# Hybrid decoder block on eight cores: own tokens' copy later, new unit orders, eight banks for the down projections

## Chip, cores and metric

One Trainium2 chip, all 8 cores, one launch. Each core computes 1024 of the 8192 token rows; nothing is exchanged between cores. The metric is the device time of the slowest core in microseconds. The engines are TensorE (PE), VectorE (DVE), ScalarE (ACT), GpSimd (POOL) and SyncE (SP); POOL and SP issue the DMAs.

## The reference

Two sequences of 4096 tokens, width 2048, one layer (cut; the causal convolutions `causal_dwconv3` have three taps):

```python
u = rmsnorm(h, ln1_g)
z = u @ w_in           # zb | zc | zv | q_lat 768 | kv_lat 512 | k_rope 64 | gates
y_conv = (zb * causal_dwconv3(zc * zv, conv_w)) @ w_conv_out
q = (rmsnorm(q_lat, q_a_g) @ w_q_b).reshape(b, s, 16, 192)
kv = (rmsnorm(kv_lat, kv_a_g) @ w_kv_b).reshape(b, s, 16, 256)   # k_nope 128 | v 128
k = concat([k_nope, broadcast(k_rope)])
q = apply_rope_tail(rmsnorm(q, q_norm_g), cos, sin)
k = apply_rope_tail(rmsnorm(k, k_norm_g), cos, sin)
y_mla = causal_attention(q, k, v) @ w_mla_out
h = h + (sigmoid(gate_a) * y_conv + sigmoid(gate_b) * y_mla) @ w_o
u = rmsnorm(h, ln2_g)
a_gate, a_up = split(causal_dwconv3(u @ w_ffn_up, ffn_conv_w) + ffn_conv_b)
h = h + (silu(a_gate) * a_up) @ w_ffn_down
```

## The kernel before

A small scheduler (`Sched`) takes operations in program order, one list per engine, and derives every semaphore wait from the buffers that an operation reads and writes. Each engine runs its list in order. That holds for the DMA issues of SP and POOL too: an issue that waits holds up what stands behind it in the list.

**Chunk stage (lines 476 to 666).** All 4096 keys of the core's sequence go through in eight groups `g` of 512. `load_x(g)` (POOL, four quarters, three buffers) brings the transposed tokens as bf16. TensorE multiplies them with the key/value input weights `wkv_sb` (loaded as f32 by four SP DMAs `wq_ops`, scaled on VectorE) into five PSUM banks `z[0]` to `z[4]`; `ssq` sums squares into `pss`, and `p2` holds the sums of the latent. The eight banks rotate, seven a group, so the next group's second bank is this group's `z[0]`. VectorE then evicts: `ea`, `fkv`, four latents `cT` (line 642), the rotary key, and the own tokens. `krss_mm(g)` (line 577), put off into the next group by `pend`, sums the rotary key's squares into the bank `p2` and copies them out on VectorE.

The own tokens of group `g` (128 of the 512) are also loaded in f32: `load_own(g)` on SP into the single buffer `xown` (`Txo`), `own_gain` multiplies by the gain in place (line 566), and line 651 writes their normalized bf16 copy into slot `7 - g` of `u_own`. `load_pos(g)` on SP fills the single buffer `posi`; `rope_tables` (line 508) reads it in its first instruction, a cast, and builds the angles for the next group in ten VectorE instructions. In group `g` SP's order before is `load_pos(g+1)`, `load_own(g+1)`; the first is free to go as soon as the cast for group `g` has read `posi`.

**Query latents (lines 673 to 709).** Three query tiles `t` = 2, 1, 0 of 260, 390 and 390 columns (two slots, three, three: tile 2 reads slots 7 and 6, tile 1 slots 5 to 3, tile 0 slots 2 to 0), six latent chunks `i` of 16 matmuls each. The sums of tile `t+1` (`qstats`) come after the first chunk of the next tile. The weight ring (`wpump`, four slots, POOL) is filled ahead of this.

**First head (lines 1051 to 1056).** `prologue_units(0)`: `KU` (512 keys: matmuls, VectorE copy, ScalarE square), `KF` (sums of squares of 2048 keys, after which the second one gives the key scale), `VU` (512 values, VectorE copy), `QA`, `QB`, `QC`, `QD` (a query tile: projections, sums, normalization). `qstats(0)` stands behind the second unit.

**Attention (lines 1061 to 1114).** 16 heads of 32 key steps, each with the score matmuls, an exponential on ScalarE, masks on POOL and the value matmuls. The 27 projection units of head h+1 are spread one a step over head h, in one PSUM bank to step 13, two from 14, three from 26; steps 2, 14 and 26 hold transposes instead. At the end of the units `u_end` releases the head's two weight blocks, and `wpump` puts the loads of two later ones on POOL.

**Convolution mixer, gates, output projection, FFN.** In the FFN `ups(g)` and `downs(g)` alternate (`FFN_ORDER`: up 0, up 1, down 0, up 2, down 1, up 3, down 2, down 3). An up pass has six projections in banks 0 to 5, then the three-tap convolution on VectorE. A down pass has 16 chunks of two halves, 11 matmuls each, in the banks `p = 6 + half`, and each half is added into `hres` by VectorE (line 1286).

Of the kernel before, what the change touches and what calls it, by code (L numbers as in the profile page):

```python
# [6 lines left out]
F32 = mybir.dt.float32  # L7
# [3 lines left out]
AF = mybir.ActivationFunctionType  # L11
# [175 lines left out]
BH = 132  # L187
# [80 lines left out]
def build_program():  # L268
# [216 lines left out]
    def load_x(g, deps=()):  # L485
        b = g % 3
        for q in range(4):
            src = xk[g * 128:(g + 1) * 128, q * 4 * NT:(q + 1) * 4 * NT].rearrange("p (k n) -> p k n", n=NT)
            S.add(POOL, lambda e, src=src, dst=xb[b][:, 4 * q:4 * q + 4, :]: e.dma_start(out=dst, in_=src),  # L489
                  writes=[Txb[b][q]], chan="x%d%d" % (b, q), extra_deps=deps)  # L490
# [9 lines left out]
    load_x(0)  # L500
# [28 lines left out]
    load_own(0)  # L529
# [35 lines left out]
    def own_gain():  # L565
        tt(xown, xown, C("g1", 0, 16).unsqueeze(2).broadcast_to([128, 16, 128]), ALU.mult, [Txo, Tcst], [Txo])

# [18 lines left out]
    own_gain()  # L586
    sqx(0, 0)
    sqx(0, 1)
    for g in range(NG):
# [51 lines left out]
        for m in range(4):  # L641
# [9 lines left out]
        tt(u_own[:, :, s * BH + 4:s * BH + BH], xown, r_[:, 0:128].unsqueeze(1).broadcast_to([128, 16, 128]),  # L651
           ALU.mult, [Txo, Tr_], [Tu[s]])
        if g + 1 < NG:
            load_pos(g + 1)
            load_own(g + 1)
            if g == 0:
                halo()
            rope_tables(posi, Tposi, NT)
            own_gain()
# [5 lines left out]
        if g == 2:  # L665
            S.add(POOL, lambda e: e.dma_start(out=msk, in_=mskd), writes=[Tmsk], chan="msk")
    load_wql(4, Twk)
    load_wql(5, Twk)
    wstate["cap"] = NSLOT
    wstate["deps"] = [S.last[DVE], S.last[ACT], S.last[PE]]  # L670
    wpump()
# [25 lines left out]
    for t in (2, 1, 0):  # L697
        b = t % 2
        off, n = QT[t]
        for i in range(6):  # L700
# [3 lines left out]
            if t == 2 and i == 0:  # L704
                pend.pop(0)()
            if i == 0 and t < 2:
                qstats(t + 1)
            act(qlatf[b][:, i, 0:n], PS[p][:, 0:n], AF.Copy, [TP[p]], [Tqlf[b][i]])
# [53 lines left out]
    for i_ in range(NPT):  # L762
        S.add(DVE, lambda e, i_=i_: e.memset(PH[i_], 1.0), writes=[TPc[i_]])
        S.add(DVE, lambda e, i_=i_: e.memset(PT[i_], 0.0), writes=[TPa[i_], TPb[i_]])  # L764
# [5 lines left out]
    later = []  # L770

# [8 lines left out]
    def prologue_units(h):  # L780
# [29 lines left out]
        def VU(g):  # L810
# [7 lines left out]
            cp(Vh[hb][:, 4 * g:4 * g + 4, 0:128], slots(PS[p], 128), [TP[p]], [TVh[hb][g]])  # L818
# [37 lines left out]
        if h == 0:  # L856
            units = [lambda: (u_start(), KU(0)), lambda: KU(1), lambda: KU(2), lambda: KU(3), lambda: VU(0),
                     lambda: KF(0), lambda: KU(4), lambda: KU(5), lambda: KU(6), lambda: KU(7), lambda: VU(1),
                     lambda: KF(1)]
            units += [lambda g=g: VU(g) for g in range(2, 8)]  # L860
            for t in (2, 1, 0):
                units += [lambda t=t: QA(t), lambda t=t: QB(t), lambda t=t: QC(t)]
            return units + [u_end]
        units.append(lambda: (u_start(), KU(0)))
        for ct in range(1, 4):
            units.append(lambda ct=ct: KU(ct))
        units.append(lambda: VU(0))
        units.append(lambda: KF(0))
        for ct in range(4, 8):
            units.append(lambda ct=ct: KU(ct))  # L870
        units.append(lambda: VU(1))
        units.append(lambda: KF(1))
        for t in range(3):
            units.append(lambda t=t: QA(t))
            units.append(lambda t=t: QB(t))
            units.append(lambda t=t: VU(2 + t))
            units.append(lambda t=t: QC(t))
        for g in range(5, 7):
            units.append(lambda g=g: VU(g))
        units.append(lambda: (VU(7), u_end()))  # L880
# [170 lines left out]
    for i_, u in enumerate(prologue_units(0)):  # L1051
        u()
        run_later()
        if i_ == 1:
# [6 lines left out]
    for si, (h, kb) in enumerate(steps):  # L1061
# [12 lines left out]
        while nq < len(steps) and nq <= si + 3:  # L1074
# [13 lines left out]
            nq += 1  # L1088
        if later:
# [183 lines left out]
    def downs(g):  # L1273
        gb = g % 2
        for c in range(16):
            wd, Twd = wget(("fd", g, c))
            h3 = slots(hres[:, c, :], BQ)
            for half in range(2):
                p = 6 + half
# [135 lines left out]
```

How the kernel before makes its waits and increments, by code:

```python
        def replay(e, eng):  # L149
            sem_e = sched.eng_sem[e]
            for o in sched.ops[e]:
                for (sem, v) in o.waits:
                    eng.wait_ge(sem, v)
                ins = o.fn(eng)
                if o.is_dma:
                    ins.then_inc(sched.chan_sem[o.chan], 16)
                elif o.needs_inc:
                    ins.then_inc(sem_e, 1)
# [18 lines left out]
            @block.sync  # L177
            def _(eng):
                replay(SP, eng)
                for ch in final_waits:
                    eng.wait_ge(sched.chan_sem[ch], 16 * sched.chan_cnt[ch])
```

## Time and profile before

| | us |
|---|---|
| median of 3 runs | 2735.43 (2735.18 to 2775.98) |
| profiled execution | 2735.31 |
| its span, slowest core (core 0) | 2733.8 |
| spans of the eight cores | 2729.8 to 2733.8 |

The span runs from the first to the last instruction. A line of the timeline has the start, the busy time and the instruction, with the count behind an x; the bracket at its end is the idle time of the engine before it and what ended it. A list of waits has the waiting engine and what it waited for, the total, the count and the longest. In a table of stretches each engine has its busy microseconds and its instructions in brackets, then the granted TensorE clock (1.00 is 2.4 GHz), the DMA engines' share and GB/s.

### The profile page before, as it was taken

Reading aid. Unit: us, or ns where it says so; the run is one execution under the profiler, and the core shown is the slowest. Engines: PE = TensorE matmul, PEld = TensorE weight load, DVE = VectorE, ACT = ScalarE, POOL = GpSimd, SP = SyncE. Lnnn points to the kernel's source line nnn. Section 1 sums busy time; section 2 is a strip of 40 time slices with the busy share of each in tenths; the row PEclk is TensorE's granted clock in tenths of the full one; section 3 lists DMA queues with packets and bytes.
Section 4 is the critical chain, followed back from the end, with each engine's and each line's share of the span. In section 5 each row is a group of like instructions: output and inputs, shape, how many; then the busy total and the mean of one; then the engine's idle time right before and its main releaser. Section 6 shows DMA issues by size and latency. Waiting matters only on the chain.

```text
span 2733.8 us, 54684 instructions; the slowest of 8 cores (2729.8 to 2733.8 us)
## 1 busy us (share of the span) xinstructions
PE 2630.4 (96%) x19779; PEld 1670.5 (61%) x19938; DVE 1241.0 (45%) x1966; ACT 844.3 (31%) x1349; POOL 505.8 (19%) x1355
## 2 busy tenths in 40 slices
PE   6998899999999999999999999999999999999999
PEld 2445566666666766666666666666665466456544
DVE  5784443443443442322211223367776277457622
ACT  3663566666666665211111111110000000000000
POOL 1100143443443433300000000000000100100010
PEclk9999999999999999999999999999999999999999
DMA  9962010010010011345444545544444444444457
GB/s 212 167 127 49 11 21 12 12 21 12 12 21 12 12 27 25 55 77 117 70 80 68 82 74 117 111 75 71 73 75 68 79 78 73 64 81 71 67 82 174
DMA packets 55268, 186.92 MB, mean 68 GB/s; under 512 B 6240, under 2 KB 6368, under 8 KB 53472
## 3 DMA queue, kind: packets, MB, share of 16 engines
q0 software_dynamic: 47088, 150.26, 34.1%
q1 hardware_dynamic: 7920, 33.15, 3.6%
q8 instruction: 168, 2.75, 0.4%
q14 instruction: 92, 0.75, 0.1%
HBM read 325.24 MB, written 8.39 MB: 122 GB/s over the span
## 4 chain that ended last, share of the span: by engine, by line
PE 91%; DVE 3%; DMA 3%; issue 2%; ACT 1%; POOL 0%; SPq 0%; DVEq 0%; ACTq 0%; POOLq 0%
PE ps L326 49%; PE pw L326 43%; DMA arena<-wkvin 1%; DVE arena L333 1%; DVE arena L350 1%; ACT arena L330 1%; DVE arena L337 1%; DMA arena<-xk 1%; DMA arena<-xo 0%; DMA outT<-arena 0%; POOL arena L347 0%; DVE arena L343 0%; DVE arena L764 0%; DVEq L153 0%; POOL arena L489 0%
## 5 line engine op out<-in xcount | busy, mean ns | idle before, releaser
L326 PE MATMUL ps<-arena 128*128 128x129 bf16 (+8 forms) x12121 | 1480.6, 275 | 64.0 <-DVE arena L350 22.4
L326 PE MATMUL pw<-arena 128*128 128x390 bf16 (+5 forms) x7658 | 1313.1, 321 | 35.3 <-DVE arena L341 21.4
L326 PEld LDWEIGHTS ps<-arena 128*128 128x128 bf16 x12202 | 967.5, 98 | 565.3 <-issue 99.8
L326 PEld LDWEIGHTS pw<-arena 128*128 128x128 bf16 x7736 | 730.7, 98 | 493.4 <-issue 41.5
L337 DVE TENSOR_TENSOR arena<-ps,arena 128x512 f32<-128x512 f32 (+6 forms) x475 | 252.7, 535 | 792.3 <-PE ps L326 714.0
L330 ACT ACTIVATE arena<-pw,arena 128x1024 bf16<-128x1024 f32 (+9 forms) x608 | 428.3, 712 | 484.5 <-PE pw L326 444.5
L330 ACT ACTIVATE arena<-arena 128x512 bf16<-128x512 bf16 (+8 forms) x381 | 269.8, 715 | 947.0 <-DVE arena L333 726.4
L397 POOL DMA_DIRECT2D arena<-wall x288 | 167.8, 583 | 1551.6 <-PE ps L326 1162.9
L347 POOL TENSOR_TENSOR arena<-arena 128x128 bf16<-128x128 bf16 (+1 forms) x1024 | 317.7, 334 | 461.6 <-ACT arena L330 459.3
L333 DVE SCALAR_TENSOR_TENSOR arena<-arena 128x1024 f32<-128x1024 f32 (+6 forms) x309 | 311.8, 1013 | 121.0 <-ACT arena L330 94.4
L350 DVE CAST arena<-ps 128x512 bf16<-128x512 f32 (+2 forms) x311 | 193.9, 634 | 260.6 <-PE ps L326 260.0
L337 DVE TENSOR_TENSOR arena<-pw,arena 128x390 f32<-128x390 f32 (+5 forms) x245 | 129.0, 555 | 140.3 <-PE pw L326 130.4
L337 DVE TENSOR_TENSOR arena<-arena 128x390 bf16<-128x390 f32 (+5 forms) x173 | 162.2, 937 | 54.1 <-ACT arena L330 32.1
L330 ACT ACTIVATE arena<-ps 128x390 bf16<-128x390 f32 (+8 forms) x215 | 99.7, 467 | 119.4 <-PE ps L326 116.1
L343 DVE TENSOR_SCALAR arena<-arena 128x1024 f32<-128x1024 f32 (+2 forms) x106 | 79.3, 748 | 1.9
L330 ACT ACTIVATE arena<-pw 128x512 bf16<-128x512 f32 (+7 forms) x60 | 29.1, 506 | 101.6 <-PE pw L326 97.8
L341 DVE TENSOR_SCALAR arena<-arena 128x390 bf16<-128x390 f32 (+7 forms) x99 | 44.8, 463 | 21.9 <-DMA arena<-wkvin 12.1
L489 POOL DMA_DIRECT2D arena<-xk x32 | 17.2, 555 | 129.0 <-PE ps L326 49.3
L330 ACT ACT_TABLE_LOAD x21 | 26.9, 1283 | 40.6 <-DVE arena L343 16.3
L350 DVE COPY arena<-ps 128x390 f32<-128x390 f32 (+2 forms) x50 | 24.4, 488 | 31.9 <-ACT arena L330 31.8
L330 ACT ACTIVATE arena<-ps,arena 128x16 bf16<-128x16 f32 x64 | 17.6, 274 | 37.4 <-PE ps L326 32.7
L341 DVE TENSOR_SCALAR arena<-ps 128x3 f32<-128x3 f32 x48 | 7.3, 152 | 25.8 <-PE ps L326 25.6
(20 smaller groups left out, 66.3 us busy)
## 6 DMA issues: line engine op xcount, KB each, us to landing
arena<-wall POOLq DMA_DIRECT2D x182, 512.0 KB, 6.7
arena<-wall POOLq DMA_DIRECT2D x64, 352.0 KB, 4.3
arena<-xk POOLq DMA_DIRECT2D x32, 512.0 KB, 16.5
arena<-xres SPq DMA_DIRECT2D x16, 520.0 KB, 5.6
arena<-xo SPq DMA_DIRECT2D x8, 1024.0 KB, 7.0
arena<-wall POOLq DMA_DIRECT2D x32, 256.0 KB, 4.9
outT<-arena SPq DMA_DIRECT2D x16, 512.0 KB, 6.4
arena<-wall POOLq DMA_DIRECT2D x16, 384.0 KB, 5.6
```

Source lines behind the costliest of these rows:

```text
L326: S.add(PE, lambda e: e.matmul(out, lhsT=lhsT, rhs=rhs, start=start, stop=stop, skip_group_check=shared), reads, writes)
L330: S.add(ACT, lambda e: e.activation(out=out, in_=in_, func=func, **kw), reads, writes)
L333: S.add(DVE, lambda e: e.scalar_tensor_tensor(out=out, in0=in0, scalar=scalar, in1=in1, op0=op0, op1=op1), reads, writes)
L337: S.add(DVE, lambda e: e.tensor_tensor(out=out, in0=in0, in1=in1, op=op), reads, writes)
L341: S.add(DVE, lambda e: e.tensor_scalar(out=out, in0=in0, scalar1=s1, scalar2=None, op0=op0), reads, writes)
L343: S.add(DVE, lambda e: e.tensor_scalar(out=out, in0=in0, scalar1=s1, scalar2=s2, op0=op0, op1=op1), reads, writes)
L347: S.add(MASK_ENG, lambda e: e.tensor_tensor(out=out, in0=in0, in1=in1, op=op), reads, writes)
L350: S.add(DVE, lambda e: e.tensor_copy(out=out, in_=in_), reads, writes)
L397: S.add(POOL, lambda e, dst=dst, src=src: e.dma_start(out=dst, in_=src), writes=[Tslot[s]], chan="w%d" % s, extra_deps=wstate["deps"] if b ...
L489: S.add(POOL, lambda e, src=src, dst=xb[b][:, 4 * q:4 * q + 4, :]: e.dma_start(out=dst, in_=src), writes=[Txb[b][q]], chan="x%d%d" % (b, q ...
```

## The change

It has five parts.

1. The quarters 2 to 4 of the first chunk wait for the weight quarter before them (`stagger`).
2. The own tokens: the row scale of group g is copied to `rown` (in ring slot 0, unused so far in this stage), and `own(g)` does gain, product and the next load two groups later; own(6) and own(7) fall into the query latents. `load_own(0)` moves from the start into group 1, the mask load from group 2 to 4, the put-off key sums from `i == 0` to `i == 2`, the first filling of the weight ring behind own(7).
3. The first head: other unit order, value copies on ScalarE, `qstats(0)` behind the fourth unit, the memsets of the `PT` buffers cut to two columns.
4. The other heads: query tiles first, then keys; the release of a head's weights at step 6 of that head itself.
5. The down projections rotate through all eight banks.

```diff
-    def load_x(g, deps=()):
+    def load_x(g, deps=(), stagger=False):
...
-                  writes=[Txb[b][q]], chan="x%d%d" % (b, q), extra_deps=deps)
+                  writes=[Txb[b][q]], chan="x%d%d" % (b, q), extra_deps=[wq_ops[q - 1]] if stagger and q else deps)
...
-    load_x(0)
+    load_x(0, stagger=True)
...
     load_pos(0)
-    load_own(0)
...
-    def own_gain():
+    rown = V(A_RING, [8, 128], F32)
+    Trown = [T() for g in range(8)]
+
+    def own(g):
+        s = 7 - g
         tt(xown, xown, C("g1", 0, 16).unsqueeze(2).broadcast_to([128, 16, 128]), ALU.mult, [Txo, Tcst], [Txo])
+        tt(u_own[:, :, s * BH + 4:s * BH + BH], xown, rown[:, g, :].unsqueeze(1).broadcast_to([128, 16, 128]),
+           ALU.mult, [Txo, Trown[g]], [Tu[s]])
+        if g + 1 < NG:
+            load_own(g + 1)
...
     rope_tables(posi, Tposi, NT)
-    own_gain()
...
         pend.append(krss_mm(g, p2))
-        tt(u_own[:, :, s * BH + 4:s * BH + BH], xown, r_[:, 0:128].unsqueeze(1).broadcast_to([128, 16, 128]),
-           ALU.mult, [Txo, Tr_], [Tu[s]])
+        cp(rown[:, g, :], r_[:, 0:128], [Tr_], [Trown[g]])
+        if g >= 2:
+            own(g - 2)
+        if g == 1:
+            load_own(0)
         if g + 1 < NG:
             load_pos(g + 1)
-            load_own(g + 1)
             if g == 0:
                 halo()
             rope_tables(posi, Tposi, NT)
-            own_gain()
...
-        if g == 2:
+        if g == 4:
             S.add(POOL, lambda e: e.dma_start(out=msk, in_=mskd), writes=[Tmsk], chan="msk")
     load_wql(4, Twk)
     load_wql(5, Twk)
-    wstate["cap"] = NSLOT
-    wstate["deps"] = [S.last[DVE], S.last[ACT], S.last[PE]]
-    wpump()
...
-            if t == 2 and i == 0:
+            if t == 2 and i == 2:
                 pend.pop(0)()
             if i == 0 and t < 2:
                 qstats(t + 1)
+            if t == 2 and i == 0:
+                own(6)
+            if t == 1 and i == 1:
+                own(7)
+                wstate["cap"] = NSLOT
+                wstate["deps"] = [S.last[DVE], S.last[ACT], S.last[PE]]
+                wpump()
...
-        S.add(DVE, lambda e, i_=i_: e.memset(PT[i_], 0.0), writes=[TPa[i_], TPb[i_]])
+        S.add(DVE, lambda e, i_=i_: e.memset(PT[i_][:, 7 * BQ:7 * BQ + 2], 0.0), writes=[TPa[i_], TPb[i_]])
...
+    ends = []
...
-            cp(Vh[hb][:, 4 * g:4 * g + 4, 0:128], slots(PS[p], 128), [TP[p]], [TVh[hb][g]])
+            if h == 0:
+                act(Vh[hb][:, 4 * g:4 * g + 4, 0:128], slots(PS[p], 128), AF.Copy, [TP[p]], [TVh[hb][g]])
+            else:
+                cp(Vh[hb][:, 4 * g:4 * g + 4, 0:128], slots(PS[p], 128), [TP[p]], [TVh[hb][g]])
...
             units = [lambda: (u_start(), KU(0)), lambda: KU(1), lambda: KU(2), lambda: KU(3), lambda: VU(0),
-                     lambda: KF(0), lambda: KU(4), lambda: KU(5), lambda: KU(6), lambda: KU(7), lambda: VU(1),
-                     lambda: KF(1)]
-            units += [lambda g=g: VU(g) for g in range(2, 8)]
+                     lambda: VU(1), lambda: KF(0), lambda: KU(4), lambda: KU(5), lambda: KU(6), lambda: KU(7),
+                     lambda: VU(2), lambda: VU(3), lambda: KF(1)]
             for t in (2, 1, 0):
-                units += [lambda t=t: QA(t), lambda t=t: QB(t), lambda t=t: QC(t)]
-            return units + [u_end]
+                units += [lambda t=t: QA(t), lambda t=t: QB(t), lambda t=t: VU(6 - t), lambda t=t: QC(t)]
+            return units + [lambda: VU(7), u_end]
...
+        units.append(lambda: (u_start(), QA(0)))
         for t in range(3):
...
+            if t:
+                units.append(lambda t=t: QA(t))
+            units += [lambda t=t: QB(t), lambda t=t: VU(t), lambda t=t: QC(t)]
+        units += [lambda ct=ct: KU(ct) for ct in range(4)] + [lambda: VU(3), lambda: KF(0)]
+        units += [lambda ct=ct: KU(ct) for ct in range(4, 8)] + [lambda: VU(4), lambda: KF(1)]
+        units += [lambda g=g: VU(g) for g in range(5, 8)]
+        ends.append(u_end)
         return units
...
-        if i_ == 1:
+        if i_ == 3:
             qstats(0)
...
+        if kb == 6 and h > 0 and ends:
+            ends.pop(0)()
...
-                p = 6 + half
+                p = (6 + 2 * c + half) % 8
```

## Rows read from the trace of the kernel before

**Rows 1.** The page: span, and busy time of each engine.

```profile
span 2733.8 us, 54684 instructions; the slowest of 8 cores (2729.8 to 2733.8 us)
PE 2630.4 (96%) x19779; PEld 1670.5 (61%) x19938; DVE 1241.0 (45%) x1966; ACT 844.3 (31%) x1349; POOL 505.8 (19%) x1355
```

**Rows 2.** Table of stretches: start:end, length, PE, PEld, DVE, ACT, POOL, PEclk, DMA.

```profile
105.25:216.16 110.91, 108.99 (x517) 49.57 (x525) 89.54 (x131) 76.64 (x80) 7.40 (x14) 1.00 0.63 129
216.16:262.45 46.29, 44.28 (x289) 28.88 (x291) 13.52 (x24) 18.04 (x42) 2.12 (x4) 0.96 0.32 48
262.45:302.25 39.80, 25.73 (x239) 16.42 (x239) 24.08 (x46) 12.64 (x26) 1.06 (x2) 0.87 0.01 2
```

**Rows 3.** TensorE's waits in attention, 302.25 to 1142 us.

```profile
PE ps L326 <- DVE arena L350: 18.4, 37, 0.8
PE ps L326 <- POOL arena L347: 4.2, 12, 1.0
```

**Rows 4.** TensorE's waits, 2089.4 us to the end (FFN from the first downs).

```profile
PE ps L326 <- DVE arena L337: 15.1, 4, 4.9
```

**Rows 5.** Timeline of VectorE, one group of the chunk stage (g = 6).

```profile
189.95 0.68 DVE L343 TENSOR_SCALAR arena<-ps 128x512 f32<-128x512 f32 x1
191.27 1.28 DVE L337 TENSOR_TENSOR arena<-pw,arena 128x512 f32<-128x512 f32 x2 [0.64 <-PE pw L326]
193.51 0.75 DVE L333 SCALAR_TENSOR_TENSOR arena<-pw,arena 128x512 bf16<-128x512 f32 x1 [0.97 <-ACT arena L330]
...
200.04 2.29 DVE L337 TENSOR_TENSOR arena<-arena 128x2048 bf16<-128x2048 f32 x1
...
211.21 0.68 DVE L343 TENSOR_SCALAR arena<-pw 128x512 f32<-128x512 f32 x1
```

**Rows 6.** Timeline of TensorE, group 1.

```profile
56.38 6.20 PE L326 MATMUL pw<-arena 128*128 128x512 bf16 x27 [0.68 <-DMA arena<-xk]
```

**Rows 7.** Timeline of all engines, end of group 2.

```profile
99.06 2.29 DVE L337 TENSOR_TENSOR arena<-arena 128x2048 f32<-128x2048 f32 x1 [5.67 <-DMA arena<-xo]
...
101.67 3.70 PE L326 MATMUL ps<-arena 128*128 128x512 bf16 x10 [3.96 <-DVE arena L350]
...
104.48 0.75 DVE L333 SCALAR_TENSOR_TENSOR arena<-ps,arena 128x512 bf16<-128x512 f32 x1 [0.97 <-ACT arena L330]
```

**Rows 8.** SP's issues at 113.4 and 113.9 us: KB, us to landing.

```profile
arena<-xo SPq DMA_DIRECT2D x1, 1024.0 KB, 6.2
arena<-posb SPq DMA_DIRECT2D x1, 256.0 KB, 6.4
```

**Rows 9.** Timelines of VectorE and TensorE, query latents.

```profile
224.27 0.16 DVE L350 COPY arena<-pw 128x4 f32<-128x4 f32 x1
231.53 4.79 PE L326 MATMUL pw<-arena 128*128 128x260 bf16 x30
```

**Rows 10.** VectorE's groups by line, 262.45 to 270 us: count, busy, mean ns, idle.

```profile
L764 DVE MEMSET arena<- 128x1040 bf16 x4 | 3.7, 925 | 0.7 <-issue 0.7
```

**Rows 11.** TensorE's waits in the first head, 262.45 to 302.25 us.

```profile
PE ps L326 <- ACT arena L330: 10.5, 5, 5.0
```

**Rows 12.** The chain of waits, the downs' restarts: start, us, what, matmuls.

```profile
2102.55 7.89 PE ps L326 x28
2110.50 10.74 PE ps L326 x49
...
2579.12 8.57 PE ps L326 x28
```

**Rows 13.** SP's issue of the constants, at 1.1 us.

```profile
arena<-cst SPq DMA_DIRECT2D x1, 230.0 KB, 3.3
```

**Rows 14.** SP's issue of positions at 87.7 us, chunk loads in flight.

```profile
arena<-posb SPq DMA_DIRECT2D x1, 256.0 KB, 15.7
```

**Rows 15.** POOL's issue of a chunk's last quarter, at 125.1 us.

```profile
arena<-xk POOLq DMA_DIRECT2D x1, 512.0 KB, 14.9
```

More of the change, by code:

```diff
@@ L857, in prologue_units @@
             units = [lambda: (u_start(), KU(0)), lambda: KU(1), lambda: KU(2), lambda: KU(3), lambda: VU(0),
-                     lambda: KF(0), lambda: KU(4), lambda: KU(5), lambda: KU(6), lambda: KU(7), lambda: VU(1),
-                     lambda: KF(1)]
-            units += [lambda g=g: VU(g) for g in range(2, 8)]
+                     lambda: VU(1), lambda: KF(0), lambda: KU(4), lambda: KU(5), lambda: KU(6), lambda: KU(7),
+                     lambda: VU(2), lambda: VU(3), lambda: KF(1)]
             for t in (2, 1, 0):
-                units += [lambda t=t: QA(t), lambda t=t: QB(t), lambda t=t: QC(t)]
-            return units + [u_end]
[L864 to L872, printed above, removed]
-        for t in range(3):
[L874 to L880, printed above, removed]
+                units += [lambda t=t: QA(t), lambda t=t: QB(t), lambda t=t: VU(6 - t), lambda t=t: QC(t)]
+            return units + [lambda: VU(7), u_end]
+        units.append(lambda: (u_start(), QA(0)))
+        for t in range(3):
+            if t:
[5 more added lines that the diff above has]
+        ends.append(u_end)
         return units
```

## The prediction

> **What bounds the kernel now.** I read the page first: TensorE is busy 96% of a 2733.8 us span [rows 1], so the change can only win back waits. TensorE's waits, listed by stage, and the table of stages then say where these are. The chunk stage (eight groups of 512 keys) ends at 216.2 us; its last 110.9 us hold 109.0 us of TensorE work, so it is full. The query-latent stage takes 46.3 us, and the first head's projections take 39.8 us with only 25.7 us of TensorE work at a granted clock of 0.87 [rows 2]. Attention hides nearly everything but 18.4 us of short waits for VectorE copies [rows 3]. The FFN has 15.1 us of waits for VectorE, nearly all of it three waits of 4.9 us [rows 4].
>
> The chunk stage is full on TensorE and almost full on VectorE. One group's VectorE work runs from 189.95 to 211.21, 21.26 us, and only 0.64 us of it waits for TensorE [rows 5]. The reader should keep that number: a group has about half a microsecond of cover.
>
> **Part 1, staggered first chunk.** The first weight quarter may land sooner, so TensorE may start sooner. But group 1 waited for the chunk x(1) itself, until 56.38 [rows 6]; x(1) is still issued behind the last weight quarter, and the same bytes come before it. I price the stagger at 0, bounds -3 and +3.
>
> **Part 2, the own tokens later: the gain.** In group 2 VectorE sits 5.67 us in front of own_gain, waiting for the own copy, and TensorE loses 3.96 us to that. The first latent of group 2 is evicted at 105.23 (104.48 + 0.75) [rows 7]. I call this eviction E2: TensorE needs that PSUM bank for the next group. After the change no own work stands there. TensorE ends group 2 at 97.71 (101.67 - 3.96), and E2 follows after the two products 1.28, ScalarE's 0.97 and the eviction 0.75 [rows 5], about 100.8. That is -4.4 us.
>
> **Part 2: the loss.** From group 2 on, own(g-2) issues the next own load on SP, and only then comes load_pos(g+1) on SP. The own load has to wait until VectorE has read xown for the last time. So positions, which before were loaded a group ahead, are now issued just as VectorE turns to rope_tables(g+1), which reads them first. Behind that cast stand, in VectorE's order, the next group's evictions, and behind those TensorE's banks. The rows show this pair in the same queue: own copy issued at 113.38, landed 6.2 us later; positions issued at 113.86, landed 6.4 us later, so 120.2 [rows 8]. Counted from the end of the u_own product, about 0.1 us before the own issue, VectorE waits 6.9 us. Before, this latency lay under the rotary tables.
>
> A VectorE period then is 21.26 - 0.64 (no more wait for TensorE) + 0.3 (the copy to rown, an estimate of mine: of its two neighbours in the rows, a 128x4 copy took 0.16 [rows 9] and a 512-column product 0.64 (1.28 for two, [rows 5])) + 6.9 = 27.8 us. The own gain and product, 2 x 2.29, only change place. The stall occurs in g = 2 to 6, so five periods, E2 to E7: 139.0 us against 110.9 [rows 2], +28.1 us. TensorE's slower restart after each wait is inside that: its 22 us fit in 27.8.
>
> **Part 2 in the query latents.** From E7 VectorE needs 5.8 us to the end of the key rotary (194.26 to 200.04 [rows 5]), 0.3 for rown, 4.6 for own(5); then the load for own(6), 6.3; own(6), 4.6; and only then the copy of the key sums, 0.2. Sum 21.8. That copy frees the bank which the sums for query tile 2 take next (bank 0, by the rotation), so these start at E7 + 22.0; before, at 231.53, E7 + 15.4 [rows 9]. That is +6.6, and after a TensorE wait of some 8 us the restart costs what the restarts in the FFN cost (below), 1.9: +8.5 us. The pop moved to i == 2 saves the wait in front of the key sums, but this bank hides that gain. own(7) ends at about E7 + 33: the load leaves at 21.7, lands at 28, the two products take 4.6. Tile 0, which reads it, starts near E7 + 37 (11 equal units remain from 22.0 in 30.9 + 1.9 us, five of them before tile 0). The four ring loads now behind own(7) have until E7 + 54.8. Both at 0; if own(7) came 5 us later still, tile 0 would pay. The mask load, two groups later on POOL, is read only in attention: 0.
>
> **Part 3, first head.** Before: four memsets of 0.93 us hold up the first key copies (3.7 us [rows 10]), and the last query tile's normalization stands between the second and third key copy; TensorE waits 10.5 us for ScalarE, 5.0 at the longest, nearly all of it in front of the key sums of squares [rows 11]. After: memsets of two columns (below a fifth of that by size, taken as 0.2), four key copies at once, value copies on ScalarE, values between the query steps. I count the 39.8 us as 25.7 of work and 14.1 of waits. Of the 10.5 all but about 1 us vanishes, which leaves 4.8, and the work loses about 1 us of slow clock: 29.5, -10.3 us. Bounds: -3.0 (the memsets alone) and -13.
>
> **Part 4, query tiles first in the other heads.** The same instructions in another order, with the release of a head's weights moved behind the next head's step 6, so POOL no longer stands there in front of the masks. At most the 18.4 us of copy waits and 4.2 us of POOL waits [rows 3] can go. The waits in front of transposes remain, since the transposes keep their steps. I take -3, bounds -10 and +22 (rivals).
>
> **Part 5, eight banks for the down projections.** With two banks TensorE must stop after two halves until VectorE, still in the last up convolution, evicts one. With eight it has 8 x 2.4 us of banks, more than the 9.6 us from the end of the ups to the restart (two halves and 4.9 us). The three waits go, 14.6 us [rows 4], and the slow restarts: 28 matmuls in 7.89 to 8.57 us where full speed gives 28 x 10.74/49 = 6.14 [rows 12], about 2.1 each, 6.4. Sum -21.0 us. The banks shared with the ups are evicted four halves before the ups return. Bounds 0 and -21.
>
> **Sum.** -4.4 + 28.1 + 8.5 - 10.3 - 3 - 21.0 = -2.1 us on 2733.8; the profiled execution took 2735.3, 1.5 us more than its span, and the median of the runs, 2735.4, agrees. Forecast **2733 us**: gains and a new wait that cancel.
>
> **Rivals.** *(A) Positions do not wait behind the own copy.* Constants of nearly the same size (230 KB) landed in 3.3 us at the start [rows 13]. Then the stall is 0.5 + 3.3 = 3.8 instead of 6.9: five times -3.1, 2718 us. Against it: positions landed 0.7 us behind the own copy in [rows 8]. The Trainium skill's page "DMA: Bandwidth & Descriptors", section "Queues, rings and completion order", says that completion on one issuing engine's queue is not first in, first out; by that rule alone A could be. It also says that each DMA engine takes its descriptors in ring order, and by that, which the row supports, it is not.
>
> *(B) The stall is covered*, as the change needs: the five periods stay at TensorE's 21.9 (109.5 of 110.9), 29.5 us less: 2704 us. Against it: half a microsecond of cover.
>
> *(C) Slower: chunk loads still in flight beside the pair.* At 87.7 positions took 15.7 us to land [rows 14], 16.3 from the product's end: 9.4 more in each of five groups, and up to 5.5 in own(6): 2786 us. It decides if the last quarter of a chunk lands after the own issue. It takes 14.9 us [rows 15] from the end of TensorE's group; the own issue comes about 18 us after that, so a margin of 3 us speaks against it.
>
> *(D) Query normalization in the wide steps*: ScalarE's two steps of about 0.5 us, three times a head, exceed what a short step leaves and stall TensorE 0.5 us each: 45 x 0.5 = 22.5 us instead of -3: 2759 us.
>
> *(E) The down projections wait for something else* (weights): 2754 us.
>
> **How the numbers follow.** Likeliest case 0.58, by itself 2718 to 2750 (the stall's 6.9 +/- 1 in five groups, the first head's -3 to -13, attention +/- 7); A 0.10, B 0.07, C 0.10, D 0.09, E 0.06. The range 2704 to 2760 leaves out most of C and part of B. 2% is 55 us, about what a measurement of this kernel can tell from no change: faster 0.01, slower 0.04 (C with D), within 0.95.
>
> **What would show it.** In the chunk stage: VectorE idle before the 512-element position cast by some 7 us with a release by the position load, in five groups, and TensorE idle once a group; E7 near 240 instead of 216. Then a TensorE wait of about 8 us in the query latents; the first head in 30 us; no 4.9 us waits in front of the downs. Without the idle time before the cast, the forecast is wrong by up to 30 us to the fast side.

## The result, and the profile after

The changed kernel takes 2770.14 us in the median of all its runs (before, beside it: 2736.35), where 2733 us (2704 to 2760) was forecast. In some executions of most kernels the cores of a die have a lower granted clock and take longer; ratios, and the times from here on, are of the other executions, and where a kernel had no others, of cores 0 to 3 alone. The ratio is 1.0097 with a 95% interval of 1.0073 to 1.0121: about 1% slower. Run again beside the experiments the kernel took 2760.3 us, ratio 1.009 (1.007 to 1.011). The slowdown is small, clear of its interval, and outside the range.

The page of the profile after, in the two lines that answer [rows 1]:

```profile
span 2770.3 us, 54863 instructions; the slowest of 8 cores (2752.5 to 2770.3 us)
PE 2671.4 (96%) x19938; PEld 1670.3 (60%) x19938; DVE 1233.1 (45%) x1966; ACT 841.5 (30%) x1357; POOL 494.3 (18%) x1355
```

The spread of the cores is new: 17.8 us against 4.0 before. Most of it comes from a clock that stood low on some pairs of cores (last section; without that, in the kernel run again, the spread is 7.7 us), so stages are compared on core 7, which shows none of it. Core 7 is the quickest of the eight here, so its +20.4 us below is less than the +24 of the slowest cores (2736 to 2760.3). Table of stretches of core 7, before and then after, cut at the same five places: the eviction that ends the eighth group (E7), the memsets that open the first head, the first score matmul, and the start of the convolution stage. Columns as in [rows 2].

```profile
0.00:215.41 215.41, 183.51 (x860) 81.44 (x860) 150.52 (x244) 126.66 (x131) 21.12 (x43) 0.98 0.82 166
215.41:263.30 47.89, 45.94 (x298) 29.66 (x299) 13.52 (x24) 18.92 (x44) 2.11 (x4) 0.96 0.32 46
263.30:301.30 38.00, 24.17 (x233) 15.57 (x231) 24.09 (x46) 11.77 (x24) 1.07 (x2) 0.87 0.03 5
301.30:1142.80 841.50, 814.34 (x8581) 570.80 (x8582) 338.43 (x671) 541.80 (x920) 336.38 (x1060) 1.00 0.12 19
1142.80:2732.10 1589.30, 1570.53 (x9971) 972.62 (x9970) 714.29 (x984) 145.10 (x231) 144.00 (x246) 0.99 0.47 84
```

```profile
0.00:233.41 233.41, 190.51 (x860) 83.15 (x860) 140.90 (x246) 127.21 (x131) 21.81 (x43) 0.95 0.73 148
233.41:288.50 55.09, 45.98 (x299) 29.28 (x299) 25.03 (x31) 18.98 (x44) 2.12 (x4) 0.94 0.25 63
288.50:311.90 23.40, 20.66 (x233) 15.03 (x231) 14.66 (x38) 15.15 (x32) 1.06 (x2) 1.00 0.07 11
311.90:1184.90 873.00, 826.70 (x8581) 565.54 (x8582) 338.20 (x671) 533.39 (x920) 324.24 (x1060) 1.00 0.10 18
1184.90:2752.50 1567.60, 1563.72 (x9971) 971.51 (x9970) 714.45 (x984) 145.04 (x231) 144.24 (x246) 1.00 0.48 85
```

The first number behind each stretch is its length. The five differences are +18.0 (chunk stage), +7.2 (query latents), -14.6 (first head), **+31.5 (attention)** and -21.7 (the rest): +20.4 us, which is core 7's 2752.5 against 2732.1. Four of the five lie within 6 us of the forecast. Attention doesn't: -3 was forecast.

**The stall in the chunk stage is there.** VectorE, group 2 of core 7 (start, us, instruction, count, idle time before it and what ended it):

```profile
106.73 4.68 DVE L337 TENSOR_TENSOR arena<-arena 128x2048 f32<-128x2048 f32 x2
117.08 0.43 DVE L350 CAST arena<-arena 128x512 f32<-128x512 int32 x1 [5.66 <-DMA arena<-posb]
```

The two instructions of `own(0)` end at 111.4, and the cast that reads the positions waits 5.66 us for them. The eviction E2, before and then after, on core 7:

```profile
103.44 0.75 DVE L333 SCALAR_TENSOR_TENSOR arena<-ps,arena 128x512 bf16<-128x512 f32 x1 [0.97 <-ACT arena L330]
```

```profile
100.06 0.75 DVE L333 SCALAR_TENSOR_TENSOR arena<-ps,arena 128x512 bf16<-128x512 f32 x1 [0.97 <-ACT arena L330]
```

The mean period from E2 to E7 is 26.5 us ((233.41 - 100.81) / 5) instead of 22.2 ((215.41 - 104.19) / 5). Core 7 is the mildest case: when the kernel ran again, the five waits were 5.5 to 7.1 us on the eight cores, and E7 came at 232.4 to 237.9. SP's two issues in that stretch (KB, us to landing) stand as in [rows 8], a little quicker:

```profile
arena<-xo SPq DMA_DIRECT2D x1, 1024.0 KB, 4.9
arena<-posb SPq DMA_DIRECT2D x1, 256.0 KB, 5.1
```

**The wait in the query latents is there**, where [rows 9] had none: VectorE's `own(6)` waits 5.47 us for its tokens, the copy of the key sums stands behind it, and TensorE waits 9.00 us for that copy.

```profile
249.49 4.69 DVE L337 TENSOR_TENSOR arena<-arena 128x2048 f32<-128x2048 f32 x2 [5.47 <-DMA arena<-xo]
254.21 0.16 DVE L350 COPY arena<-pw 128x4 f32<-128x4 f32 x1
```

```profile
254.52 5.77 PE L326 MATMUL pw<-arena 128*128 128x260 bf16 x28 [9.00 <-DVE arena L350]
```

**Attention.** TensorE's waits in attention of core 7 after, the answer to [rows 3] (waits for whom: total, count, longest):

```profile
PE ps L326 <- DVE arena L350: 18.7, 48, 1.1
PE ps L326 <- DVE arena L337: 13.7, 41, 1.5
PE ps L326 <- ACT arena L330: 7.3, 30, 0.8
PE ps L326 <- POOL arena L347: 2.8, 7, 1.0
```

On this core the list before has the two rows of [rows 3], and 1.8 us each for L337 and for ScalarE. So POOL's 4.2 us became 2.8, and the waits for VectorE's products (L337) and for ScalarE grew from 3.6 to 21.0. TensorE's groups by tile shape say before which matmuls the waits stand (count, busy, mean ns, idle before them and whom it waited for). After:

```profile
L326 PE MATMUL ps<-arena 128*128 128x128 bf16 x2048 | 139.2, 219 | 14.8 <-DVE arena L337 13.4
L326 PE MATMUL ps<-arena 128*128 128x390 bf16 x484 | 95.1, 327 | 11.7 <-DVE arena L350 7.7 <-ACT arena L330 3.6
L326 PE MATMUL ps<-arena 128*128 128x260 bf16 x242 | 34.4, 273 | 9.2 <-DVE arena L350 6.2 <-ACT arena L330 2.9
```

and before:

```profile
L326 PE MATMUL ps<-arena 128*128 128x128 bf16 x2048 | 139.8, 219 | 16.8 <-DVE arena L350 13.4 <-ACT arena L330 1.8 <-DVE arena L337 1.5
L326 PE MATMUL ps<-arena 128*128 128x390 bf16 x484 | 96.8, 332 | 0.5 <-DVE arena L350 0.5
L326 PE MATMUL ps<-arena 128*128 128x260 bf16 x242 | 34.5, 273 | 0.0
```

Before the 128 column matmuls the wait only changed its name, from the copies (L350) to the products (L337), and went from 16.8 to 14.8 us. The 390 and 260 column matmuls are the query projections and their sums. They waited 0.5 us in all before and 20.9 us after: these waits are the new ones. One head after, TensorE, around the first query tiles of the next head:

```profile
589.96 1.61 PE L326 MATMUL ps<-arena 128*128 128x390 bf16 x14 [0.20 <-ACT arena L330]
591.41 0.93 PE L326 MATMUL pw<-arena 128*128 128x512 bf16 x4
592.61 1.60 PE L326 MATMUL ps<-arena 128*128 128x390 bf16 x14 [0.27 <-DVE arena L350]
594.05 0.82 PE L326 MATMUL pw<-arena 128*128 128x512 bf16 x4
595.24 1.51 PE L326 MATMUL ps<-arena 128*128 128x128 bf16 x24 [0.36 <-DVE arena L337]
```

and ScalarE, then VectorE, for the second of these waits:

```profile
590.35 1.00 ACT L330 ACTIVATE arena<-pw,arena 128x910 bf16<-128x910 f32 x1
591.25 0.48 ACT L330 ACTIVATE arena<-ps 128x390 bf16<-128x390 f32 x1
```

```profile
591.90 0.56 DVE L350 COPY arena<-ps 128x390 f32<-128x390 f32 x1 [0.26 <-ACT arena L330]
```

Read it in order. The query product was in its bank by 591.57 at the latest (589.96 + 1.61). ScalarE was in an exponential until 591.35; its square of the product ends at 591.73; VectorE's copy of the same bank is let in only then, 591.90, and ends at 592.46. The next unit uses the same bank, since until step 13 of a head there is only one, and starts at 592.61. The scheduler orders every two users of a bank, so two readers on two engines take turns.

### The profile page after: what moved, and what is told of

It is laid out like the page before. It is cut to its first block, busy times and chain, and to the rows that moved or that the text cites. A ratio compares the mean times of both kernels' runs of the same rounds, so it can differ in the third digit from the quotient of the medians.

```text
span 2770.3 us, 54863 instructions; the slowest of 8 cores (2752.5 to 2770.3 us)
## 1 busy us (share of the span) xinstructions
PE 2671.4 (96%) x19938; PEld 1670.3 (60%) x19938; DVE 1233.1 (45%) x1966; ACT 841.5 (30%) x1357; POOL 494.3 (18%) x1355
## 4 chain that ended last, share of the span: by engine, by line
PE 84%; DVE 6%; ACT 4%; issue 3%; DMA 2%; POOL 0%; DVEq 0%; ACTq 0%; SPq 0%; POOLq 0%
PE pw L326 44%; PE ps L326 39%; ACT arena L330 4%; DVE arena L337 3%; DVE arena L350 1%; DVE arena L333 1%; DMA arena<-posb 1%; DMA arena<-xk 1%; DMA arena<-wkvin 0%; POOL arena L347 0%; DVE arena L341 0%; DVE arena L343 0%; DVEq L153 0%; ACTq L153 0%; DMA arena<-xo 0%
## 5 line engine op out<-in xcount | busy, mean ns | idle before, releaser
L326 PE MATMUL pw<-arena 128*128 128x390 bf16 (+9 forms) x8434 | 1500.6, 329 | 44.1 <-DVE arena L341 15.8
L326 PE MATMUL ps<-arena 128*128 128x129 bf16 (+7 forms) x11504 | 1341.1, 269 | 50.9 <-DVE arena L350 20.6
L326 PEld LDWEIGHTS ps<-arena 128*128 128x128 bf16 x11504 | 895.0, 98 | 492.6 <-issue 150.4
L326 PEld LDWEIGHTS pw<-arena 128*128 128x128 bf16 x8434 | 803.4, 98 | 603.0 <-issue 105.2
L337 DVE TENSOR_TENSOR arena<-ps,arena 128x260 f32<-128x260 f32 (+6 forms) x413 | 210.6, 511 | 713.9 <-PE ps L326 611.6
L347 POOL TENSOR_TENSOR arena<-arena 128x128 bf16<-128x128 bf16 (+1 forms) x1024 | 303.8, 320 | 522.0 <-ACT arena L330 520.4
L350 DVE CAST arena<-ps 128x384 bf16<-128x384 f32 (+2 forms) x305 | 192.3, 635 | 226.3 <-PE ps L326 223.6
L337 DVE TENSOR_TENSOR arena<-pw,arena 128x390 f32<-128x390 f32 (+5 forms) x307 | 172.6, 586 | 230.5 <-PE pw L326 216.3
L337 DVE TENSOR_TENSOR arena<-arena 128x390 bf16<-128x390 f32 (+7 forms) x173 | 155.7, 900 | 49.1 <-ACT arena L330 30.1
L489 POOL DMA_DIRECT2D arena<-xk x32 | 18.8, 596 | 144.8 <-PE ps L326 60.5
L350 DVE COPY arena<-ps 128x390 f32<-128x390 f32 (+2 forms) x51 | 25.0, 490 | 37.0 <-ACT arena L330 36.3
L350 DVE CAST arena<-arena 128x512 f32<-128x512 int32 (+3 forms) x27 | 10.8, 401 | 42.4 <-DMA arena<-posb 34.6
```

Of the source, the lines that this page charges most:

```text
L326: S.add(PE, lambda e: e.matmul(out, lhsT=lhsT, rhs=rhs, start=start, stop=stop, skip_group_check=shared), reads, writes)
L337: S.add(DVE, lambda e: e.tensor_tensor(out=out, in0=in0, in1=in1, op=op), reads, writes)
L347: S.add(MASK_ENG, lambda e: e.tensor_tensor(out=out, in0=in0, in1=in1, op=op), reads, writes)
L350: S.add(DVE, lambda e: e.tensor_copy(out=out, in_=in_), reads, writes)
```

## Experiments

**1. Which part costs attention its time.** Two parts undone one at a time in the changed kernel, and both together. The keys-first order of before in heads 1 to 15, with the later release kept:

```diff
-        units.append(lambda: (u_start(), QA(0)))
+        units.append(lambda: (u_start(), KU(0)))
+        for ct in range(1, 4):
+            units.append(lambda ct=ct: KU(ct))
...
         for t in range(3):
...
+            units.append(lambda t=t: QA(t))
...
         ends.append(u_end)
```

> The changed kernel with the old order of the projection units in heads 1 to 15 (keys first); the release of the weights at step 6 stays. Theory A (the query units, first in the wide steps with one bank, hold that bank through ScalarE's square, queued behind the exponential, and then VectorE's copy, so the next unit waits): attention, from the first score matmul of head 0 to that of the convolution stage, goes from 873 us (core 7 of the changed kernel) back to 841 +/- 4, and the kernel gains about 31 us. Theory B (the later release, whose loads on POOL now stand among the masks of step 6 and after, is what costs): attention stays near 870.

Measured: 2723.4 us (2725.26 in the median of all executions), ratio 0.9969 (0.9943 to 0.9996); attention 836.5 to 837.7 us on cores 0, 1, 4 and 7. The later release is still in this kernel, so it isn't what costs.

The positions loaded ahead of `own(g-2)`:

```diff
+        if g + 1 < NG:
+            load_pos(g + 1)
         if g >= 2:
             own(g - 2)
...
         if g + 1 < NG:
-            load_pos(g + 1)
```

> The changed kernel with the load of the next positions issued on SP ahead of the own tokens' step instead of behind it. Theory A (VectorE's 5.7 to 7.2 us in front of the position cast, five times, are the queue behind the own load, and they set the group's period of 26.5 us): those waits go, the period returns to TensorE's 21.9, five periods save 23 us; the wait of some 8 us for the key sums in the query latents stays. Theory B (the period is set by TensorE's restarts at low clock after each wait): the waits for positions go but the period stays above 24. The clock: if the dips to a granted 0.81 follow restarts of TensorE, fewer restarts make them rarer and the spread of the cores smaller.

Measured: 2735.5 us, ratio 0.999 (0.9976 to 1.0005). The cast follows `own(0)` without a wait (VectorE, group 2; compare the pair above):

```profile
108.71 4.68 DVE L337 TENSOR_TENSOR arena<-arena 128x2048 f32<-128x2048 f32 x2
113.30 0.42 DVE L350 CAST arena<-arena 128x512 f32<-128x512 int32 x1
```

All five periods are 21.9 us on every core and E7 lies at 212.3 on core 7; attention stays at 873 to 876 us.

Both together:

> Both repairs, old unit order in heads 1 to 15 and positions ahead of the own step. If the two losses are independent they add: 23 + 31 = 54 us less than the changed kernel, about 2700 us on an undisturbed core, 1.2% faster than the kernel before. If one hides the other, the sum is smaller.

Measured: 2699.16 us, ratio 0.9862 (0.984 to 0.9885). The last four stretches of core 7, cut as above:

```profile
211.62:266.30 54.68, 45.95 (x298) 29.31 (x299) 25.05 (x30) 18.98 (x44) 2.11 (x4) 0.94 0.34 81
266.30:289.70 23.40, 20.66 (x233) 15.03 (x231) 14.67 (x38) 15.15 (x32) 1.06 (x2) 1.00 0.06 10
289.70:1126.10 836.40, 809.50 (x8581) 569.28 (x8582) 338.31 (x671) 540.39 (x920) 336.61 (x1060) 1.00 0.13 19
1126.10:2693.80 1567.70, 1563.75 (x9971) 971.53 (x9971) 714.41 (x984) 145.01 (x231) 144.24 (x246) 1.00 0.53 85
```

The two causes add: the order costs 36.3 us (2735.5 - 2699.2), the late positions 24.2 (2723.4 - 2699.2), 60.5 together, and with both undone the changed kernel is 61.1 us quicker (2760.3 - 2699.2). Undone, the changed kernel is 1.4% faster than the one before. The shape table of this kernel has the query matmuls' waits back at nothing:

```profile
L326 PE MATMUL ps<-arena 128*128 128x390 bf16 x484 | 95.1, 327 | 0.5 <-DVE arena L350 0.5
L326 PE MATMUL ps<-arena 128*128 128x260 bf16 x242 | 34.5, 273 | 0.0
```

**2. What holds the bank.** In the changed kernel, VectorE copies the query's nope product first and ScalarE squares the copy:

```diff
-            act(sqn[:, 0:n], PS[p][:, 0:n], AF.Square, [TP[p]], [Tsqn])
             cp(qraw[:, 0:n], PS[p][:, 0:n], [TP[p]], [Tqraw])
+            act(sqn[:, 0:n], qraw[:, 0:n], AF.Square, [Tqraw], [Tsqn])
```

> The changed kernel, query units still first, but in QA the copy of VectorE goes first and ScalarE squares that copy in SBUF, so that the bank is free after the copy alone. Theory A (the bank is held by square and copy one after the other): TensorE's waits in front of QB, three a head of 0.3 to 0.5 us, go, those behind QB and QC stay; attention falls by some 8 to 12 us from 873. Theory C (ScalarE is simply too full in the wide steps, whichever operand it reads): attention stays within 3 us of 873.

Measured: 2750.79 us, ratio 1.0054 (1.0034 to 1.0074); attention 862.7 us, 10 to 12 less than the changed kernel's 873 to 875. Then also the rope product, multiplied by VectorE first and squared from its bank after that:

```diff
-            act(sqr[:, 0:n], PS[p][:, 0:n], AF.Square, [TP[p]], [Tsqr])
             tt(qrc[:, 0:n], PS[p][:, 0:n], CSq[:, off:off + n], ALU.mult, [TP[p]] + TCq, [Tqrc])
+            act(sqr[:, 0:n], PS[p][:, 0:n], AF.Square, [TP[p]], [Tsqr])
```

> The changed kernel with VectorE ahead of ScalarE on both query products of a head: the nope product copied out first and squared from SBUF, the rope product multiplied first and then squared from its bank. Theory: in the wide steps one bank serves the units, and what holds it is ScalarE's turn followed by VectorE's; with VectorE first its turn runs while ScalarE still works off exponentials. Attention 862.7 us with the first half of this falls by another 6 to 10 us, to 853 to 857, and the time to some 2743 us, ratio 1.0025. Rival: the bank is held until ScalarE comes to it whatever the order, and attention stays at 860 to 863 us.

Measured: attention 860.6 us, 2.1 less; the rival's number. (Of this kernel and of e7_release, e9_nostagger and e11_best in experiment 5 cores 0 to 3 are compared: here the slowest of them took 2745.8 to 2748.5 us, before beside it 2732.4 to 2735.7.) TensorE's waits in attention, core 0:

```profile
PE ps L326 <- ACT arena L330: 17.3, 60, 0.8
PE ps L326 <- DVE arena L350: 9.4, 22, 1.1
PE ps L326 <- DVE arena L337: 4.8, 11, 1.5
```

The waits changed their name. VectorE's product (L337) fell from 13.7 to 4.8 and ScalarE's rose from 7.3 to 17.3: who reads last has the wait. So ScalarE was taken off these banks altogether: VectorE copies both products and the sums of squares out, and ScalarE works from SBUF (the nope product as in the first step).

```diff
...
-            act(sqr[:, 0:n], PS[p][:, 0:n], AF.Square, [TP[p]], [Tsqr])
-            tt(qrc[:, 0:n], PS[p][:, 0:n], CSq[:, off:off + n], ALU.mult, [TP[p]] + TCq, [Tqrc])
+            cp(qbr[:, 0:n], PS[p][:, 0:n], [TP[p]], Tsqk[2:4])
+            act(sqr[:, 0:n], qbr[:, 0:n], AF.Square, Tsqk[2:4], [Tsqr])
+            tt(qrc[:, 0:n], qbr[:, 0:n], CSq[:, off:off + n], ALU.mult, Tsqk[2:4] + TCq, [Tqrc])
...
-            rsqrt_act(rstdqh[:, 0:n], PS[p][:, 0:n], 192.0, [TP[p]], [Trstdqh], rstdqh[:, 0:n], Trstdqh)
+            cp(rstdqh[:, 0:n], PS[p][:, 0:n], [TP[p]], [Trstdqh])
+            rsqrt_act(rstdqh[:, 0:n], rstdqh[:, 0:n], 192.0, [Trstdqh], [Trstdqh], rstdqh[:, 0:n], Trstdqh)
```

> The changed kernel with ScalarE taken off the units' banks in heads 1 to 15 and the first: VectorE copies every query product and the sums of squares out of PSUM, and ScalarE squares and takes the root from SBUF (three more VectorE instructions of 0.4 to 0.6 us per head's tile, 45 tiles). Theory: in the order of the changed kernel the single bank of the wide steps waits for ScalarE, which is behind an exponential; without it TensorE's waits on ScalarE in attention fall from 17.3 us to under 5, those before the 390 and 260 column products from 11.1 to a few, and attention from 860.6 to 845 to 852 us; time some 2733 us. Rival: a single bank costs its wait whichever engine empties it, VectorE's waits grow instead, and attention stays at 856 us or above.

Measured: 2737.5 to 2741.2 us on the six cores with an undisturbed clock, where the changed kernel's spans are 2751.5 to 2759.2; attention 852.9 to 854.2 us on all eight, between the two expectations. From core 5, two rows of the waits, then two of the shapes:

```profile
PE ps L326 <- DVE arena L350: 26.9, 43, 1.4
PE ps L326 <- ACT arena L330: 0.8, 1, 0.8
```

```profile
L326 PE MATMUL ps<-arena 128*128 128x390 bf16 x484 | 96.1, 330 | 5.0 <-DVE arena L350 5.0
L326 PE MATMUL ps<-arena 128*128 128x260 bf16 x242 | 34.6, 273 | 12.4 <-DVE arena L350 12.4
```

Of the order's 36 us, 19 to 21 go when ScalarE leaves the banks, and some 17 stay (853.5 against 836.5) with VectorE alone, the cost of its two added instructions a tile among them (the expectation counts three, but the first copy was there before). So ScalarE behind its exponentials is about half of the cause; the other half is at most what one bank costs units that need long emptying, whoever does it. That these 17 us would go with a second bank in the wide steps wasn't tried: the seven others are in use there.

**3. The gains alone.** Eight banks for the down projections in the kernel before, nothing else:

```diff
-                p = 6 + half
+                p = (6 + 2 * c + half) % 8
```

> The kernel before with nothing changed but the banks of the down projections, p = (6 + 2c + half) % 8. Theory: the tail falls from 1589.3 to 1567.6 us as in the changed kernel, nothing else moves: 2714.5 us, ratio 0.992. Rival: part of the tail's gain came from the layout of the rest (the later release, other weight loads in flight): a fall of 10 us or less, ratio 0.996 or above.

Measured: 2714.27 us, ratio 0.9921 (0.9901 to 0.994), 21.9 us less. This part depends on no other.

**4. What the second part is worth when repaired.** In the kernel of both repairs, the own tokens as before:

```diff
-        cp(rown[:, g, :], r_[:, 0:128], [Tr_], [Trown[g]])
+        tt(u_own[:, :, s * BH + 4:s * BH + BH], xown, r_[:, 0:128].unsqueeze(1).broadcast_to([128, 16, 128]),
+           ALU.mult, [Txo, Tr_], [Tu[s]])
...
-        if g >= 2:
-            own(g - 2)
...
+            load_own(g + 1)
```

> The repaired kernel with the whole second part undone: own tokens loaded, gained and written as in the kernel before, positions beside them; stagger, first head's order, later release and eight banks stay. Theory: the second part's gain of 4.5 us at the end of the latents (211.6 against 216.2) is eaten by the 8.6 us wait of the key sums, so undoing it costs nothing: 2697 us, memsets 2 us earlier than in the repaired kernel. Rival: the early own tokens were worth their 4.5 us or more: 2703 us or above.

Measured: 2693.18 us, ratio 0.9844 (0.9827 to 0.9861): 6.0 us better without the second part. The intervals of the two ratios overlap, but every execution of this kernel (at most 2693.5 us) is below every one of the kernel of both repairs (at least 2697.9). In the mean of the eight cores the second part brings E7 2.2 us forward, and loses 8.3 in the query latents and 2.0 in attention; why in attention, no run shows. And the second part kept, but `own(6)` moved behind the put-off key sums:

```diff
-            if t == 2 and i == 0:
+            if t == 2 and i == 3:
                 own(6)
```

> The repaired kernel (keys first, positions loaded ahead of the own step) with own(6) moved behind the put-off key sums: from the first to the fourth of the first query tile's six latents. Theory: the 8.6 us that TensorE stood in the query latents was the key sums' bank, copied out by VectorE only behind own(6), which itself waited 5.1 us for its tokens. It goes, with some 1 us of restart behind it: 2691 us (ratio to the repaired kernel's 2699 about 0.997). Rival: the wait moves to own(7), whose tokens are now loaded 5 us later and which the last query tile reads: 2697 to 2699.

Measured: 2695.3 us, ratio 0.9852 (0.9833 to 0.9872), 3.9 us better, again with intervals that overlap and executions (at most 2695.9) that don't. The 8.6 us wait goes and 5.8 us of it come back in front of tile 0, now for `own(7)`, as the rival had it (TensorE, core 7):

```profile
242.02 6.04 PE L326 MATMUL ps<-arena 128*128 128x390 bf16 x22 [5.77 <-DVE arena L337]
```

**5. Smaller questions.** The changed kernel again, beside the others:

> The changed kernel itself again, beside the others. Theory: 2760 us where no pair of cores shows a lowered granted clock (spans 2752 to 2759), ratio 1.009; attention 872 to 876 us on every core. If the lowered clock of some pairs belongs to the kernel's stalls in the latents, most runs show it and lie at 2764 to 2775; if it belongs to the chip or to chance, few do, as in the two experiments that kept those stalls.

Measured: 2760.3 us, spans 2751.5 to 2759.2, clock 0.992 to 0.995 on all cores, attention 873.3 to 874.9 us. The release of the weights back at the end of the units, in the kernel of both repairs:

```diff
-        for g in range(5, 8):
+        for g in range(5, 7):
             units.append(lambda g=g: VU(g))
-        ends.append(u_end)
+        units.append(lambda: (VU(7), u_end()))
```

> The repaired kernel (keys first, positions ahead of the own step) with the two weight tiles of a head given back at the end of its units again, as in the kernel before. Theory: the repaired kernel's attention of 836.5 us lies 5 us under the 841.5 us of the kernel before because of the later release alone, so it returns to 841 to 842 us and the time to 2704 us, ratio 0.988. Rival: the release is worth nothing and the 5 us come from the first head (its value copies on ScalarE and its later query tiles): 836 to 838 us, 2699 us.

Measured: attention 838.5 to 840.3 us against 836.4 to 837.8; the slowest of cores 0 to 3 took 2699.6 to 2700.4. Between the two expectations: the later release is worth 2 to 3 us. The first chunk's transfers started together again (`load_x(0)` without `stagger`), in the kernel of both repairs:

> The repaired kernel with the first chunk's four transfers started at once again. Theory: TensorE starts 4 to 5 us later but waits 3 to 7 us less inside group 0, so the first latent is evicted at 51 to 53 us as now and the time stays: 2699 us, within 3. Rival: the second group's end, 79 to 81 us, moves with it, by 2 us or more either way.

Measured: 2695.0 to 2698.2 us on the slowest of cores 0 to 3. On these cores TensorE starts at 19.6 to 21.1 us instead of 15.9 to 16.7, and E7 lies at 207.9 to 211.6 against 211.6 to 213.0. The stagger is worth nothing; if anything, it costs 1 us. Last, VectorE ahead of ScalarE on the query products (as in experiment 2) with keys first and the own tokens as before:

> Keys first, own tokens as in the kernel before, stagger, first head's order, later release, eight banks (2693 us, attention 835 us), and VectorE ahead of ScalarE on both query products of a head. Theory: with keys first the query products come where the steps are narrow and several banks are free, so the order of the two readers is worth little: attention 833 to 836 us, 2691 to 2694 us, ratio 0.984. Rival: VectorE's 18 us of waits in attention are the square and copy here too: attention 825 us, 2683 us.

Measured: 2690.6 to 2691.9 us on the slowest of cores 0 to 3, against 2690.5 to 2691.9 of the same kernel without it: no difference. Attention is 2 to 3 us shorter (832.3 to 834.0), and the first head 2.3 us longer.

## Why the prediction was wrong

The medians make a ledger. Before 2736.2; eight banks -21.9; first head, release and stagger together -21.1 (2693.2); the own tokens later, positions in time, +6.0 (2699.2); positions late +24.2; query tiles first +36.3. Sum 2759.7, measured 2760.3.

**The failed step is Part 4**, "I take -3, bounds -10 and +22". It argued that the same instructions in another order can at most win back waits, and it priced the waits that were there [rows 3]. It didn't ask in which steps the moved units would then run, and that is where the price lies: query units moved from steps with two or three banks into those with one. The account of the kernel before has that fact (one bank to step 13, two from 14, three from 26), and the prediction used it nowhere. Rival D, with a chance of 0.09, saw the place, the short steps, and ScalarE. It priced 45 x 0.5 us of ScalarE time, 22.5, where the runs show 36: 22.5 is near the 19 to 21 us that went when ScalarE left the banks, and the 17 us or so that stayed, with one bank and VectorE alone, are in no term of the sum. TensorE also pays twice for a stop, in idle and in busy time. On core 7 its idle time in attention grew from 27.2 us (841.50 - 814.34) to 46.3, and its busy time from 814.3 to 826.7 for the same 8581 matmuls. Of +31.5, idle time is 19.1 and busy time 12.4. The single matmuls did not get longer (327 ns against 332 with 390 columns, 273 and 273 with 260), so what is lost is their overlap. That it is lost behind stops is how I read it: a matmul behind a stop has no earlier one to overlap with. The Trainium skill's page "TensorE: Matmul & The Clock Gate", section "Step-by-step: what each phase is for", says the same of the drain of a lone matmul; no run here measured it by itself. It does not go by the number of stops alone: the last kernel of experiment 2 is busy 817.9 us on core 5 with 65 waits, both repairs 809.5 with 49, the changed kernel 826.7 with 127.

**Part 2 was right in kind.** The stall was there in five groups, on core 7 5.7 us instead of 6.9; periods of 26.5 instead of 27.8; E7 18.0 us later, forecast 23.7 (28.1 - 4.4). The positions did land just behind the own copy (5.1 and 4.9 us), so rival A falls. Rival B falls with the period, rival C too (positions took 5.1 us, not 15.7). The Trainium skill's page "DMA: Bandwidth & Descriptors", section "Queues, rings and completion order", doesn't promise completion in the order of issue; here the landings came in that order (4.9 us after the first issue, 5.1 after the second). The query latents lost 7.2, forecast 8.5, by the bank that was named. E2 came at 100.81 on core 7 (forecast, for core 0, 100.8), 3.4 us earlier than before on that core instead of 4.4, but that gain is small change: repaired, Part 2 still costs 6 us, since it puts more in front of the key sums than it takes from group 2, or with `own(6)` moved in front of tile 0.

**Part 3** gained 14.6 on core 7 where 10.3 was forecast, just past its bound of -13: 2.7 us of waits are left (23.40 - 20.66) instead of 4.8, and the work is 20.7 us instead of 24.7, since its granted clock is 1.00, no longer 0.87 (24.2 us before on this core, times 0.87, is 21.0). The slow clock was a term of 1 us and gave back 3.5. **Part 5** gained 21.7 (21.9 alone), forecast 21.0, so rival E falls. **Part 1**: 0, as priced.

The sum then: forecast -2.1, core 7 +20.4. The difference of 22.5 is Part 4's +34.5, less 5.7 in the chunk stage, 4.3 in the first head, 1.3 in the query latents and 0.7 in the downs. The range reached to 2760, and the undisturbed kernel takes 2760.3. That D's 2759 lies so close is luck: its attention term is 9 us too small on core 7 (22.5 against 31.5), and the other stages came out 12 us under the forecast (-11.1 against +0.9). Three slips in the sums are small: the waits left in the first head come to 4.6 (14.1 - 9.5), not 4.8; E2's terms add to 100.7; and a restart in the FFN is 1.9 in one place and 2.1 in another.

## What to carry to other kernels

When units of work change places, look up what each place offers (banks, buffers, slack of every engine in that step), and price the units at their new place; the waits of the old order say nothing about it. Where every two users of a PSUM bank are ordered, as here, a bank read by two engines is held for both turns one after the other, and the first turn starts only when that engine's queue lets it: give such units the steps with spare banks, and the steps with one bank to units that one quick copy empties. When a load is moved behind another on one queue, count from its issue to its reader; a gain of 3.4 us in one group came with a loss of 4.3 us in each of five, undone by exchanging two lines.

## What was not expected of the hardware

In the first runs of the changed kernel the cores of some pairs show a granted clock that is neither of the two levels (1.2 and 2.4 GHz, 0.5 and 1 in these tables). Table of stretches of core 1 after:

```profile
55.00:190.00 135.00, 132.93 (x513) 54.11 (x512) 80.78 (x139) 75.78 (x77) 10.91 (x19) 0.80 0.69 124
```

It stands at 0.81 from 37 to 199 us on cores 0 and 1, and from 133 to 295 us on cores 4 and 5, some 162 us each, but for one fall to the lower level inside; E7 comes at 249.27 on core 1 instead of 233.41 on core 7. In the run shown these pairs have a mean clock of 0.984 and 0.985, and core 1 sets the time. TensorE had just restarted from the lower level where most of them begin, but in the first kernel of experiment 1 cores 6 and 7 show one from 2570 us on, with no restart near. The changed kernel showed it in most of its first runs and, when it ran again, on no core of the profiled run, with the same stalls and the same ratio (1.0097 and 1.009); the last kernel of experiment 2 shows it on cores 2 and 3, and the kernel before once had the four cores of a die at a mean of 0.984 to 0.987. So it isn't the cause of the slowdown, and what sets it off stays open. The page "TensorE: Matmul & The Clock Gate" of the Trainium skill (section "Seeing it yourself") knows a limit of 13/16, 0.81, for a whole die under load. In the run shown it took pairs of cores, while the other pair of the die had no 0.81.
